# Operands of 512-column products begin at 64 instead of 128 modulo 256 bytes

## What is computed

```python
h = concatenate([meta, x])                      # 528 x 1024
for i in range(2):                              # first block, two layers
    xn = rms_norm(h, attn_norm[i])
    h = h + concatenate([gla(xn @ w_in), forgetting_attention(xn @ w_in)]) @ w_out[i]
    h = h + conv_ffn(rms_norm(h, ffn_norm[i]), w_up[i], conv_w[i], conv_b[i], w_down[i])
x = rms_norm(h, final_norm)[:, 16:]             # the real tokens alone
h = concatenate([meta_2, x])                    # second block, one layer
a = rmsnorm(h, norm_mix_g)
y_attn = dsa_attention(top 128 keys of an index score) @ w_attn_out
y_conv = (cb * short_conv(cc * cu)) @ w_conv_out
h = h + (sigmoid(ga) * y_attn + sigmoid(gb) * y_conv) @ w_out
h = h + (silu(f @ w_gate) * (f @ w_up)) @ w_down       # f = rmsnorm(h), width 2816
return rmsnorm(h, norm_final_g)[:, 16:]
```

## Time and profile before

| what | value |
|---|---|
| median of 3 runs | 2213.65 us (2213.56 to 2213.66) |
| span of the profiled execution | 2212.6 us |
| TensorE matmuls, busy | 2187.9 us, 99% of the span |
| weight loads, busy | 2006.8 us, 91% |
| VectorE busy | 1423.7 us, 64% |
| ScalarE busy | 1069.1 us, 48% |
| GpSimd busy | 148.2 us, 7% |
| granted TensorE clock, mean | 0.999 |

### The profile page before, as it was taken

How to read it: one execution, slowest core, us unless ns; L and a number is a source line. 1 busy time by engine, 2 the same in 40 slices (tenths; PEclk the granted TensorE clock), 3 DMA queues, 4 the chain that set the end, 5 groups by cost and what they waited for, 6 DMA issues and landing times.

```text
span 2212.6 us, 39479 instructions
## 1 busy us (share of the span) xinstructions
PE 2187.9 (99%) x15711; PEld 2006.8 (91%) x15711; DVE 1423.7 (64%) x2661; ACT 1069.1 (48%) x2027; POOL 148.2 (7%) x245
## 2 busy tenths in 40 slices
PE   9999999999999999999999999999999999999998
PEld 8799999999997899998899889978899888998997
DVE  5356689559744466887498567869444465863664
ACT  5356556347533465555377534232344444552652
POOL 4111111000000011100000010101000000000001
PEclk9999999999999999999999999999999999999999
DMA  6656678686335546664354273777512222443651
GB/s 209 181 150 163 185 198 234 190 243 177 128 94 155 162 114 168 182 184 149 123 175 157 81 188 101 204 196 216 148 66 67 67 95 92 152 159 120 184 168 51
DMA packets 104737, 336.15 MB, mean 152 GB/s; under 512 B 14966, under 2 KB 19036, under 8 KB 102252
## 3 DMA queue, kind: packets, MB, share of 16 engines
q1 hardware_dynamic: 90460, 227.30, 31.5%
q0 software_dynamic: 13376, 105.03, 20.4%
q10 hardware_dynamic: 720, 1.31, 0.2%
HBM read 331.46 MB, written 102.79 MB: 196 GB/s over the span
## 4 chain that ended last, share of the span: by engine, by line
PE 92%; DVE 4%; ACT 2%; issue 1%; DMA 0%; POOL 0%; SPq 0%; ACTq 0%; DVEq 0%; POOLq 0%
PE G L1485 55%; PE G L1522 17%; PE G L1601 7%; PE X L1522 3%; PE X L1822 1%; DVE wL L2499 1%; PE X L1909 1%; PE X L1774 1%; PE X L1798 1%; ACT wH L1962 1%; PE X L1893 1%; PE X L1561 1%; PE X L1878 1%; PE X L1485 1%; PE X L1865 0%
## 5 line engine op out<-in xcount | busy, mean ns | idle before, releaser
L1962 ACT ACTIVATE wH<-raw 128x512 fp32r<-128x512 f32 (+3 forms) x741 | 492.2, 685 | 436.2 <-PE G L1485 354.8
L2499 DVE TENSOR_TENSOR wL<-raw,wH 128x512 fp32r<-128x512 f32 (+3 forms) x741 | 555.9, 763 | 219.3 <-ACT wH L1962 216.4
L1485 PE MATMUL G<-aH,wH 128*128 128x264 f32 (+3 forms) x1744 | 445.6, 318 | 3.5 <-DVE aL L2512 2.8
L1485 PE MATMUL G<-aH,wL 128*128 128x264 f32 (+3 forms) x1744 | 427.4, 308 | 0.0
L1485 PE MATMUL G<-aL,wH 128*128 128x264 f32 (+3 forms) x1744 | 427.3, 308 | 0.0
L1485 PEld LDWEIGHTS G<-aH,wH 128*128 128x128 f32 (+1 forms) x1744 | 284.5, 188 | 23.5 <-DVE aL L2512 3.2
L1485 PEld LDWEIGHTS G<-aH,wL 128*128 128x128 f32 (+1 forms) x1744 | 282.8, 188 | 16.3
L1485 PEld LDWEIGHTS G<-aL,wH 128*128 128x128 f32 (+1 forms) x1744 | 283.1, 188 | 13.0 <-issue 0.2
L1522 PE MATMUL G<-seven,wH 128*128 128x256 f32 (+2 forms) x1152 | 213.1, 284 | 2.8 <-DVE wL L2499 1.5
L2660 DVE TENSOR_TENSOR hT<-G,hT 128x528 f32<-128x528 f32 (+1 forms) x83 | 58.0, 698 | 199.4 <-PE G L1485 199.1
L1522 PEld LDWEIGHTS G<-seven,wH 128*128 128x128 f32 x1152 | 177.9, 189 | 5.3 <-issue 2.9
(11 more groups left out here) (412 smaller groups left out, 3967.7 us busy)
## 6 DMA issues: line engine op xcount, KB each, us to landing
raw<-weights SPq DMA_DIRECT2D x179, 512.0 KB, 4.3
weight_sums<-weights POOLq DMA_DIRECT2D x72, 704.0 KB, 6.4
raw<-weight_sums SPq DMA_DIRECT2D x192, 256.0 KB, 3.0
raw<-weights SPq DMA_DIRECT2D x145, 256.0 KB, 2.9
raw<-weights SPq DMA_DIRECT2D x48, 704.0 KB, 4.2
weight_sums<-weight_sums POOLq DMA_DIRECT2D x24, 704.0 KB, 4.8
weight_sums<-weights POOLq DMA_DIRECT2D x24, 512.0 KB, 5.3
weight_sums<-weights POOLq DMA_DIRECT2D x24, 448.0 KB, 5.0
```

The lines of the kernel that those rows point to most:

```text
L1485: done = e.matmul(m.pair(i)[0:M, bank, 0:n], a[:, k, 0:M], b[:, kx, lo - t0:lo - t0 + n], start=(k == 0 and c == 0), stop=(k == nk - 1 and ...
L1962: e.activation(m.high(i)[:, c], m.raw(i)[:, c], ACT.Copy).then_inc(s.w_hi, 1)
L2499: e.tensor_tensor(m.low(i)[:, c], m.raw(i)[:, c], m.high(i)[:, c].bitcast(F32), ALU.subtract).then_inc(s.w_lo, 1)
```

## The change

A second pair of views of the same memory is added, `bH` and `bL`. They begin 48 elements (192 bytes) further into each slice of `aH` and `aL`, so that token 0 is at 0 modulo 256 and token 16 at 64. The second block's products (list `BLOCK2`) and all that writes their operands use these views; the first block stays on `aH` and `aL`. The other tiles are shifted by padding, and `real_high` and `real_low` by 16 elements, so that each begins at 64 modulo 256.

```diff
+BLOCK2 = ("ki", "qi", "cu", "cc", "cb", "vv", "gb", "dk", "dq", "ga", "ya", "u2", "g2")
...
+        self.bH, self.bL = high[:, :, 48:STRIDE], lows[:, :, 48:STRIDE]
...
-            self.real_high = flat(self.hidH[:, :, :])[:, 32:32 + 11 * 512].rearrange("p (k t) -> p k t", k=11)
+            self.real_high = flat(self.hidH[:, :, :])[:, 16:16 + 11 * 512].rearrange("p (k t) -> p k t", k=11)
...
-            self.real_low = flat(self.hidL[:, :, :])[:, 48:48 + 11 * 512].rearrange("p (k t) -> p k t", k=11)
+            self.real_low = flat(self.hidL[:, :, :])[:, 32:32 + 11 * 512].rearrange("p (k t) -> p k t", k=11)
...
-                sb("front_att", [128, 32], F32, c1)
+                sb("front_att", [128, 16], F32, c1)
...
-                sb("front_z", [128, 16], F32, c1)
...
+                sb("front_q2", [128, 48], F32, c1)
...
+                sb("front_m", [128, 48], F32, c1)
...
-            sb("front_hid", [128, 32], F32, c)
+            sb("front_hid", [128, 16], F32, c)
...
-        return m.aH, m.aL, 0
+        return (m.bH, m.bL, 0) if role[0] in BLOCK2 else (m.aH, m.aL, 0)
...
+        ah, al, _ = operand(role, 0)
...
-            for q, (a, b) in enumerate(((m.aH, wh), (m.aL, wh), (m.aH, wl))):
+            for q, (a, b) in enumerate(((ah, wh), (al, wh), (ah, wl))):
...
-        operand_high(m.aH[:, j, t0:L], m.hT[:, j, t0:L], m.vc(key if len(key) == 2 else "ffn2", j))
+        high = m.bH if key == ("ffn2",) else m.aH
+        operand_high(high[:, j, t0:L], m.hT[:, j, t0:L], m.vc(key if len(key) == 2 else "ffn2", j))
```

More of the change, by code:

```diff
@@ L1323, in __init__ @@
                 scratch = [sb("scratch0", [128, 11, 512], F32, c1), sb("scratch1", [128, 11, 512], F32, c1)]
-            sb("front_hid", [128, 32], F32, c)
+            sb("front_hid", [128, 16], F32, c)
             self.hid2H = sb("hid2H", [128, 11, 512], F32R, c)
             self.hid2L = sb("hid2L", [128, 11, 512], F32R, c)
-            sb("behind_hid", [128, 32], F32, c)
+            sb("behind_hid", [128, 48], F32, c)
             self.U = sb("U2", [128, 2, 512], F32, c)
@@ L2045, in prepmid @@
         h, meta = m.hT[:, j, NM:L], m.hT[:, j, 0:NM]
-        e.activation(m.aH[:, j, NM:L], h, ACT.Copy, scale=m.gains[:, j:j + 1]).then_inc(*own.one())
-        operand_high(m.aH[:, j, 0:NM], meta, m.vc("mix2", j))
+        e.activation(m.bH[:, j, NM:L], h, ACT.Copy, scale=m.gains[:, j:j + 1]).then_inc(*own.one())
+        operand_high(m.bH[:, j, 0:NM], meta, m.vc("mix2", j))
         e.activation(m.xm[:, j, 0:NM], meta, ACT.Copy, scale=m.vc("mix2", j)).then_inc(s.meta_in, 1)
@@ L2295, in attin @@
             e.wait_ge(s.chunk, AT["ga", 7] + 1)
-        operand_high(m.q2H[:, h, :] if h < 2 else m.aH[:, h, NM:L], m.attnT[:, h, :], 1.0)
+        operand_high(m.q2H[:, h, :] if h < 2 else m.bH[:, h, NM:L], m.attnT[:, h, :], 1.0)
     def gla(l, bk):
@@ L2518, in prep @@
         t0 = NM if key == ("ffn2",) else 0
-        operand_low(("prep", key, j), m.aL[:, j, t0:L], m.hT[:, j, t0:L], m.vc(key if len(key) == 2 else "ffn2", j),
-                    m.aH[:, j, t0:L])
+        high, low = (m.bH, m.bL) if key == ("ffn2",) else (m.aH, m.aL)
+        operand_low(("prep", key, j), low[:, j, t0:L], m.hT[:, j, t0:L], m.vc(key if len(key) == 2 else "ffn2", j),
+                    high[:, j, t0:L])
     def prepmid(j):
@@ L2526, in prepmid @@
         e.wait_ge(s.a_hi, OPERAND["prepmid", j])
-        e.scalar_tensor_tensor(out=m.aL[:, j, NM:L], in0=h, scalar=m.gains[:, j:j + 1], in1=m.aH[:, j, NM:L].bitcast(F32),
+        e.scalar_tensor_tensor(out=m.bL[:, j, NM:L], in0=h, scalar=m.gains[:, j:j + 1], in1=m.bH[:, j, NM:L].bitcast(F32),
                                op0=ALU.mult, op1=ALU.subtract).then_inc(*own.one())
-        e.scalar_tensor_tensor(out=m.aL[:, j, 0:NM], in0=meta, scalar=m.vc("mix2", j), in1=m.aH[:, j, 0:NM].bitcast(F32),
+        e.scalar_tensor_tensor(out=m.bL[:, j, 0:NM], in0=meta, scalar=m.vc("mix2", j), in1=m.bH[:, j, 0:NM].bitcast(F32),
                                op0=ALU.mult, op1=ALU.subtract).then_inc(s.a_lo, 1)
@@ L2548, in attin @@
         e.wait_ge(s.a_hi, OPERAND["attin", h])
-        high, low = (m.q2H[:, h, :], m.attL[:, h, :]) if h < 2 else (m.aH[:, h, NM:L], m.aL[:, h, NM:L])
+        high, low = (m.q2H[:, h, :], m.attL[:, h, :]) if h < 2 else (m.bH[:, h, NM:L], m.bL[:, h, NM:L])
         e.tensor_tensor(low, m.attnT[:, h, :], high.bitcast(F32), ALU.subtract).then_inc(s.a_lo, 1)
```

## The result

The changed kernel is slower: 2228.64 us, the median of 5 runs (2228.28 to 2229.35), against 2213.65 us for the kernel before in as many runs. The ratio is 1.0067, with a 95% interval of 1.0057 to 1.0078. The forecast was 2205.0 us, the range ended at 2218, and slower had a chance of 0.18. The profiled span went from 2212.6 to 2226.6 us, 14.0 more.

A forecast was written before the change was run, and what follows sets the result against it. TensorE was taken to bound the kernel; 8.4 us from 512-column products plus 0.2 from the last product's halves, off 2213.65, gave 2205.0 us. The range was 2197 to 2218 us.

The forecast's parts named there:

- The bound: Whole kernel: TensorE, busy 2187.9 of 2212.6 us, sets the time; a matmul's gain or loss goes to the end nearly one to one.
- The count: High-high products and their two siblings: 2655 matmuls of 512 columns go from 128 to 64 modulo 256.
- the place of the first difference in pace: Layer 1's `down` products were to be the first stretch to gain, with the two traces alike up to there.
- the price: 512-column matmuls moved from 128 to 64: each gains 3.15 ns, priced from 256-column rows; 119.8 ns at 128 against 116.65 at 64.
- The term of -3.15 ns on 2655 matmuls: All 512-column products moved to 64: 8.4 us off the time, with bounds of 4.0 and 14.9 us.
- The mean of 116.65 ns: Seven-product stage, 256 columns at 64: mean of 115.0 and 118.3 ns a matmul, taken as the step at 64.
- C: 512-column operands at 64 pay for straddling one more stretch: 3.3 ns each, 9.0 us slower, 2222.7 us; chance 0.18.
- A: The beginning does not matter at 512 columns: time stays 2213.65 us, give or take 1.8; chance 0.29.
- B: Gain grows with length, from collision with other reads: 512 columns gain twice what 256 do, 16.9 us, 2196.7 us; chance 0.10.
- The halves: The last product's 66 matmuls of 256 columns, moved from 128 to 64: 0.2 us gained, bounds 0.1 and 0.4.
- The shorter products of the second block: 768 matmuls of 258 columns and 432 of 264: taken as 0, with 1 ns each way, 1.2 us.
- `vv`: 192 matmuls whose stationary side moves: 0.6 us either way, taken as 0.

The follow-up runs named there:

- the kernel with the `down` products alone: The kernel before with only layer 1's 528 down matmuls of 512 columns moved to begin at 64: 2217.25 us against 2213.85, ratio 1.0016.
- the alternating case: Bare matmuls without the model, moving operand at 128 and 64 in turn, weights at 128: 227.0 ns a step at 512 columns, 116.8 at 256.
- the run on lengths: Bare matmuls without the model, four beginnings, lengths 128 to 496 with weights at 128, then moved weights; at 496 columns 220.2 ns at 64, 223.3 at 128.
- the sixteen beginnings: Bare matmuls without the model, sixteen moving beginnings, weights at 128: 233.1 ns at 64 and 227.5 at 128 for 512 columns, 113.8 and 120.0 for 256.
- the short runs: Bare matmuls without the model, weights at 128, stretches at 64 with other beginnings between: 114.6 or 117.5 ns at 256 columns, 233.1 to 233.7 at 512.

## Why the prediction was wrong

**The bound was right.** TensorE set the time and its idle time did not grow (24.7 to 23.8 us, the 0.9 at the program's start), the clock stayed, and VectorE's and ScalarE's busy times kept within 1.3 us. The 528 matmuls of the `down` products show it best: what they lose one by one is what the whole kernel loses.

**The count was right** (2655), and so was the place of the first difference in pace, layer 1's `down` products. (The 0.9 us of the program's start come before it and stand in the kernel with the `down` products alone too.)

**The step that failed** is the price: "the overhead is paid once per matmul and depends on its beginning, not on its length". I took it from one coincidence, 13.1 ns of overhead at 128 for both 256 and 512 columns, and then let 256-column rows at 64 stand for 512-column matmuls at 64. At 128 the overhead is indeed the same. At 64 it is 113.6 - 106.7 = 6.9 ns at 256 columns and 233.3 - 213.3 = 20.0 ns at 512. The term of -3.15 ns on 2655 matmuls was +6.5 ns in steady runs, and +5.7 ns on average over all of them (15.2 us on 2655). Two rows cannot show that a quantity is independent of the length when both are at the same beginning; the row that was missing is one at another beginning.

The rows at 64 also hid something. By the order of products in `by_seven`, the twelve matmuls from 2059.86 are product 7 and those from 2064.09 product 3; I had the names exchanged. The mean of 116.65 ns stays. But with the names right, one product at one address takes 118.3 ns in the stage and 114.2 at its end, and the second pace stood in the trace of the kernel before.

What I also left out is the second operand. I kept "the same weights at 128" as a constant of the comparison. It is half of the cause: moved along with the moving operand, it restores 226.8 ns.

**The rivals.** C had the right side, the right place and the right condition, a step over 226.4 ns, but not its reason. It priced straddling at 3.3 ns; the step rose by 6.5 to 6.9. And straddling is not it: 2048 bytes touch nine stretches of 256 bytes from 128 as well as from 64, so only stretches of 128 bytes would set the two apart; and with weights at 64 the operand that straddles in the same way has 227.1 ns. The objection that I held against C, that the 256-column runs are faster at 64, is true and proves nothing for 512 columns. A (no difference at 512 columns) is refuted. B (gain grows with the length) had the sign wrong; that other reads are involved, its reason, has support from the runs with moved and with narrower weights.

**The small terms.** The halves: 0.2 us foreseen, 0.3 found. The shorter products of the second block: 0, with 1 ns allowed each way, foreseen; 0.0 us in sum found, but by luck: 0.9 ns less on each of the 258-column matmuls and 1.8 ns more on each of the 264-column ones cancel. `vv`: 0 foreseen, 0.0 found. The range failed since its upper end was drawn through a small price for C: C at its measured price, 14 to 15 us, would have needed 2229.

The Trainium skill's rule on reads within lines of 16 bytes (SBUF — State Buffer, "Specifications") stood for A, and doesn't tell 64 from 128; here they differ by 6.5 ns in steady runs. And a sentence of the Trainium skill that I had not weighed speaks of the mechanism itself: TensorE: Matmul & The Clock Gate, "Step-by-step: what each phase is for", says that TensorE has two independent read ports, so that loading the next weights does not take read bandwidth from the running matmul. These runs sit badly with the conclusion, though they do not measure bandwidth: with the moving operand fixed at 128, moving the weights alone from 128 to 64 changes a 512-column step from 227.5 to 229.2 ns, and moving them to 0 makes it 232.5.

**What stays open.** Why the distance of the two beginnings matters, why its sign turns between 496 and 512 columns, why a moving operand that begins at 128 and 64 in turn has the level pace at 512 columns, and why two paces exist at 256 columns. A collision between the reads of weights and of the moving operand fits the runs with moved and with narrower weights, but was not shown by itself, and the alternating case does not follow from it in any simple form. Which neighbours keep a short run of 512 columns from settling was not tried either.

## What to carry to other kernels

Price an address for exactly the number of columns that it will be used with: the best beginning for 256 columns (64 bytes below the weights, 114 ns against 120) was the worst for 512 (233 against 227). Look at both operands of a matmul and compare their beginnings modulo 256 bytes; for long runs of 512 columns keep them level. Where TensorE is 99% busy, some nanoseconds a matmul are worth a small kernel of bare matmuls that sweeps the beginnings in one run: its settled steps, 226.8 and 233.3 ns, are those of the whole kernel, and their difference times the 528 `down` products is the 3.4 us that these cost. Let each case run long enough to settle, and check that the clock is up before the first one.

## What the runs showed of the hardware

- Starts of `float32r` matmuls of 512 columns lie 226.7 to 234.5 ns apart at a granted clock of 2.4 GHz, by where the two operands begin. The spacing of 215.7 ns that the Trainium skill gives (TensorE: Matmul & The Clock Gate, "Wait — 56ns, not 53.3ns?") was seen in no run here; the steady rows come no nearer than 226.7.
- Two paces at equal addresses, 113.3 and 117.7 ns, each stable over hundreds of matmuls, and changed after a stretch with a wait of 0.18 us or after one matmul at another beginning.
- By their steps, `float32r` matmuls of 128 columns, each with its own weights, ran at the lower clock for 61 us of unbroken work. In the timeline of the run on lengths, at its start (the cases of 128 columns at 128 and at 192 lie between the first row and the second):

```profile
53.17 10.44 PE L56 MATMUL P<-at064x,w128x 128*128 128x128 f32 x48
...
83.89 8.26 PE L56 MATMUL P<-at000x,w128x 128*128 128x192 f32 x48
91.99 5.52 PE L56 MATMUL P<-at064x,w128x 128*128 128x192 f32 x48
97.35 5.53 PE L56 MATMUL P<-at128x,w128x 128*128 128x192 f32 x48
```

  The step is 30.72 / 144 = 213.3 ns at 128 columns and 5.36 / 48 = 111.7 ns in the second case of 192. But the length is not the reason. The first case of 192 columns takes 8.10 us: its first 25 steps after the change take 213.3 ns too, and from 89.5 us on they take 112. The trace's record of the granted clock, 1.00, begins at 89.56 us. (The view prints 1.00 for the time before it as well, for which there is no record.) In the other bare kernels the record begins where the step drops too: in the sixteen beginnings at 45.1 us, where 512 columns go from 427 to some 232 ns, and in the short runs at 21.6 us, where 256 columns go from 213.3 to 113.3. 427 and 213.3 ns are 512 and 256 columns at 1.2 GHz, so the cases of 128 columns ran at that level.
- So, at 1.2 GHz, 128, 192 and 256 columns all have a step of 213.3 ns. At 2.4 GHz, 192 columns have 111.7 ns in the run on lengths, against 113.3 to 120 for 256: a shorter operand saves little there. No run shows 128 columns of `float32r` at 2.4 GHz.
